# A hybrid decoder layer with experts: a token's expert weights formed in the projection stage, stored beside its row and gathered with it

## The reference

```python
x = _layer_norm(ALPHA * x + (1.0 + g1[:, None]) * mix, ln1_g, ln1_b)
u2 = x * (1.0 + sc2[:, None]) + sh2[:, None]
# _hier_moe, un = u2 as rows
p_group = softmax(g_logits); g_sel = argmax(g_logits)
top_v, top_i = lax.top_k(e_sel, TOP_K)            # e_sel: logits of the chosen group
top_w = softmax(top_v) * take_along_axis(p_group, g_sel[:, None], axis=1)
comb = one_hot(g_sel)[:, :, None] * w_in_group[:, None, :]   # n_tok x 16, two entries not zero
h = jax.nn.silu(hg) * hu * comb[:, :, None]
y = jnp.einsum('nef,efd->nd', h, w_down)
x = _layer_norm(ALPHA * x + (1.0 + g2[:, None]) * y_moe, ln2_g, ln2_b)
```

## Time and profile before

| | us |
|---|---|
| median of 3 runs (lowest, highest) | 1300.3 (1299.82, 1301.27) |
| the profiled execution | 1304.18 |
| its span, first to last instruction | 1302.2 |
| PE busy | 1182.5 (91%) |
| DVE busy | 920.2 (71%) |
| ACT busy | 500.9 (38%) |
| POOL busy | 358.5 (28%) |
| mean granted clock of PE | 0.956 of full speed |

### The profile page before, as it was taken

The page is one execution under the profiler, slowest core; times in us unless marked ns, Lnnn a source line. Parts: engine busy times, 40 slices in busy tenths (PEclk is TensorE's granted clock), DMA queues, the critical chain, the costliest instruction groups (busy, mean ns, idle before and its releaser), DMA issues.

```text
span 1302.2 us, 23073 instructions
## 1 busy us (share of the span) xinstructions
PE 1182.5 (91%) x6683; PEld 963.3 (74%) x6684; DVE 920.2 (71%) x1821; ACT 500.9 (38%) x934; POOL 358.5 (28%) x447
## 2 busy tenths in 40 slices
PE   6889999999999489999997379999999999999495
PEld 2378988988999478888785368888888888888242
DVE  2764988888898689898899875457655745432298
ACT  0525335444533432111111334446544644422175
POOL 1411202212220431211120053344445544332100
PEclk9979999999999699999999589999999999999798
DMA  8814224404413455344333568877998789854673
GB/s 337 293 41 168 66 96 161 141 20 161 161 53 110 150 171 179 130 163 159 130 121 130 182 232 234 236 221 204 302 272 241 211 246 286 250 129 76 211 279 153
DMA packets 112561, 231.44 MB, mean 178 GB/s; under 512 B 11735, under 2 KB 70363, under 8 KB 109419
## 3 DMA queue, kind: packets, MB, share of 16 engines
q1 hardware_dynamic: 98691, 180.50, 39.6%
q0 software_dynamic: 13824, 50.34, 16.5%
HBM read 161.49 MB, written 69.97 MB: 178 GB/s over the span
## 4 chain that ended last, share of the span: by engine, by line
PE 69%; DVE 17%; issue 5%; ACT 4%; DMA 3%; POOL 1%; SPq 1%; DVEq 0%; ACTq 0%; POOLq 0%
PE bank L1599 19%; PE bank L1601 19%; PE bank L1600 19%; PE bank L1552 5%; DMA ada_arena<-in_w_ada 2%; PE bank L1687 2%; DVE ada_arena L1533 2%; PE bank L1573 2%; PE bank L1620 1%; DVE arena L1252 1%; PE bank L1774 1%; DVE ada_arena L1519 1%; DVE st L1255 1%; PE bank L1629 1%; DVE arena L1268 1%
## 5 line engine op out<-in xcount | busy, mean ns | idle before, releaser
L1599 PE MATMUL bank<-parts 128*128 128x256 f32 (+2 forms) x1472 | 513.3, 349 | 38.6 <-ACT arena L775 20.9
L1601 PE MATMUL bank<-parts 128*128 128x256 f32 (+2 forms) x1472 | 496.4, 337 | 0.0
L1600 PE MATMUL bank<-parts 128*128 128x256 f32 (+2 forms) x1472 | 495.9, 337 | 0.0
L1599 PEld LDWEIGHTS bank<-parts 128*128 128x128 f32 x1472 | 283.0, 192 | 82.6 <-ACT arena L775 29.1
L1601 PEld LDWEIGHTS bank<-parts 128*128 128x128 f32 x1472 | 282.7, 192 | 28.6
L1600 PEld LDWEIGHTS bank<-parts 128*128 128x128 f32 x1472 | 283.4, 193 | 25.5
L1552 PE MATMUL bank<-ident,arena 128*128 128x128 f32 (+4 forms) x788 | 116.4, 279 | 14.3 <-DMA arena<-u_d,tok_i 5.8
L1552 PEld LDWEIGHTS bank<-ident,arena 128*128 128x128 f32 (+4 forms) x788 | 94.5, 145 | 39.8 <-issue 9.2
L1442 DVE TENSOR_TENSOR parts<-arena,parts x90 | 105.0, 1221 | 15.9 <-ACT parts L942 14.2
L1454 DVE TENSOR_TENSOR arena<-arena,bank 128x256 f32<-128x256 f32 x48 | 20.1, 419 | 132.3 <-ACT arena L952 131.2
L647 POOL TENSOR_TENSOR arena<-arena 128x256 f32<-128x256 f32 (+1 forms) x36 | 26.1, 728 | 267.9 <-DVE h_last L1181 190.0
(11 more groups left out here) (266 smaller groups left out, 1761.3 us busy)
## 6 DMA issues: line engine op xcount, KB each, us to landing
arena<-in_w_ada SPq DMA_DIRECT2D x16, 1024.0 KB, 8.4
arena<-in_w_gate SPq DMA_DIRECT2D x16, 1024.0 KB, 5.9
arena<-in_w_up SPq DMA_DIRECT2D x16, 1024.0 KB, 12.7
arena<-in_w_down SPq DMA_DIRECT2D x16, 1024.0 KB, 14.5
y_d<-zero SPq DMA_DIRECT2D x17, 512.0 KB, 6.4
ada_arena<-in_w_ada SPq DMA_DIRECT2D x4, 2048.0 KB, 15.4
arena<-in_x_prompt SPq DMA_DIRECT2D x8, 1024.0 KB, 7.8
yT_d<-arena SPq DMA_DIRECT2D x16, 512.0 KB, 4.6
```

Source lines behind the costliest of these rows:

```text
L1599: pe.matmul(out, x_hi, w_hi, start=start, stop=False)
L1600: pe.matmul(out, x_hi, w_lo, start=False, stop=False)
L1601: return pe.matmul(out, x_lo, w_hi, start=False, stop=stop)
```

## The change

A token's 16 expert weights (`comb`, two of them not zero) are formed batch by batch by DVE: `weigh(n)` right after `choose(n)`, the Exp of both softmaxes on ACT in one instruction, and `weights_of(n)` before `rows_of(n)` (for batch 3, which now takes tiles 13 to 16, after it). POOL stores `comb` to DRAM in 16 new columns beside each row of u2, in two DMAs, and waits for both before the first gather. A gathered row has 1040 elements. ACT, in `x_evac`, reads the slot's expert number and copies the one column of `xg` that belongs to it into `wslot` (`w_now`); both `y_evac` wait for that, and so does the gather that overwrites the buffer. `plain_rows`, the three bf16 parts, POOL's three multiplications, PE's 68 matmuls and DVE's sums go. ACT's loop over the tiles of the projection stage is written out. SP stores zeros into the 16 columns of the 128 spare rows. The diff, without plain renaming and address changes:

```diff
+WEIGH = ((0, 4), (4, 5), (9, 4), (13, 4))
...
-        u2_d = nc.dram_tensor("u2_d", [P + NTOK, D], F32).ap()
+        u2_d = nc.dram_tensor("u2_d", [P + NTOK, D + NE], F32).ap()
...
-        prod_w = ada_at(18432, 2, NT, NE)
+        prod_w = ada_at(28300, 2, 5, NE)
...
-        hot_b = at(19072, 2 * NT * SLOTS).bitcast(BF16).rearrange("p (k t v s) -> p k t v s", k=2, t=NT, v=2)
...
+        comb = ada_at(24832, NT, NE)
...
+            sp.dma_start(u2_d[0:P, D:D + NE], zero[:, 0:NE]).then_inc(S["junk_in"], 16)
...
+            pool.wait_ge(S["comb_ok"], len(WEIGH))
+            pool.dma_start(u2_d[P:P + SEQ, D:D + NE].rearrange("(t p) e -> p t e", p=P), comb[:, 0:NT - 1, :]).then_inc(S["comb_st"], 16)
+            pool.dma_start(u2_d[P + SEQ:P + NTOK, D:D + NE], comb[0:NS, NT - 1, :]).then_inc(S["comb_st"], 16)
             pool.wait_ge(S["idx_ready"], 1)
...
-            pool.wait_ge(S["junk_in"], 16)
+            pool.wait_ge(S["junk_in"], 32)
+            pool.wait_ge(S["comb_st"], 32)
             for s in range(2):
                 pool.indirect_dma_start(out=xg[s], out_offset=None, in_=u2_d,
                                         in_offset=bass.IndirectOffsetOnAxis(ap=tok_i[:, s:s + 1], axis=0)).then_inc(S[f"xg{s}"], 16)
-            pool.wait_ge(S["wpart_ready"], 1)
-            by_tok = lambda v: v.unsqueeze(3).to_broadcast([P, 2, NT, SLOTS])
-            for v in range(2):
-                o.did(pool.tensor_tensor(hot_b[:, :, :, v, :], hot_s, by_tok(w_part[v]), ALU.mult))
-            o.wait()
-            pool.tensor_tensor(hot_s, hot_s, by_tok(w_part[2]), ALU.mult).then_inc(S["hotw_ready"], 1)
             for s in (2, 3):
                 pool.wait_ge(S["xgT_mm"], 2 * s - 2)
+                pool.wait_ge(S["w_now"], s - 1)
                 gather(s, s % 2)
...
-            with act.Fori(1, NT // 2 - 1) as j:
-                for b in range(2):
-                    u2T_evac(2 * j + b - 2)
-                    split_y(2 * j + b + 2, b, j + 2)
-                    deviation(2 * j + b, b)
+            def weigh(n):
+                act.wait_ge(S["w_exp"], n + 1)
+                act.activation(exp_in[:, 0:5 * WEIGH[n][1]], exp_in[:, 0:5 * WEIGH[n][1]], ACT.Exp).then_inc(S["w_expd"], 1)
+            for t in range(2, NT - 3):
+                u2T_evac(t - 2)
+                split_y(t + 2, t % 2, t // 2 + 2)
+                deviation(t, t % 2)
+                if t - 1 in CHOOSE_AT:
+                    weigh(CHOOSE_AT.index(t - 1))
             u2T_evac(NT - 5)
             split_y(NT - 1, 0, NT // 2 + 1, NS)
             deviation(NT - 3, 0)
             u2T_evac(NT - 4)
             deviation(NT - 2, 1)
+            weigh(2)
             u2T_evac(NT - 3)
             deviation(NT - 1, 0, NS)
             u2T_evac(NT - 2)
@@ -918,16 +926,12 @@
                 act.activation(u2T[:, 4 * h:4 * h + 4, 0:NS], bank[4 + h][:, :].rearrange("p (k n) -> p k n", n=P)[:, :, 0:NS],
                                ACT.Copy).then_inc(S["u2T_ok"], 1)
+            weigh(3)
...
-            act.wait_ge(S["w_exp"], 1)
-            act.activation(g_dif, g_dif, ACT.Exp).then_inc(S["w_expd"], 1)
-            act.wait_ge(S["w_exp"], 2)
-            act.activation(d_12, d_12, ACT.Exp).then_inc(S["w_expd"], 1)
...
-            def x_evac(s):
+            def x_evac(s, b):
+                e = act.value_load(slot_ei[0:1, 0, ds(s, 1)], min_val=0, max_val=NE - 1)
                 for h in range(2):
                     act.wait_ge(S["xgT_mm"], 2 * s + h + 1)
+                    if h == 0:
+                        act.activation(wslot[:, ds(s, 1)], xg[b][:, ds(e + D, 1)], ACT.Copy).then_inc(S["w_now"], 1)
...
+                act.wait_ge(S["w_now"], s + 1)
...
-            act.wait_ge(S["wslot_ok"], 1)
...
-            def plain_rows(n):
-
-                t0, nt = BATCHES[n]
-                for t in range(t0, t0 + nt):
-                    for k in range(2):
-                        o.did(dve.tensor_scalar(hot_a[:, k, t, :], iota_r[:], pos_f[:, k, t:t + 1], None, ALU.is_equal))
+            def weigh(n):
+                t0, nt = WEIGH[n]
+                tiles = slice(t0, t0 + nt)
+                gl, el = logits[:, tiles, 0:NGR], logits[:, tiles, NGR:NR]
+                g_dif, d_12 = exp_in[:, 0:NGR * nt].rearrange("p (t g) -> p t g", g=NGR), exp_in[:, NGR * nt:5 * nt]
+                o.did(dve.tensor_tensor(prod_w[:, :, 0:nt, :], e_all[:, :, tiles, :], el.unsqueeze(1).to_broadcast([P, 2, nt, NE]), ALU.mult))
+                o.step(dve.tensor_reduce(g_max[:, 0:nt], gl, axis=AX, op=ALU.max))
+                o.did(dve.tensor_tensor(g_dif, gl, bc(g_max[:, 0:nt], NGR), ALU.subtract))
+                o.step(dve.tensor_reduce(m_12[:, :, 0:nt], prod_w[:, :, 0:nt, :], axis=AX, op=ALU.add))
+                dve.tensor_tensor(d_12, m_12[:, 1, 0:nt], m_12[:, 0, 0:nt], ALU.subtract).then_inc(S["w_exp"], 1)
+            def weights_of(n):
+                t0, nt = WEIGH[n]
+                tiles = slice(t0, t0 + nt)
+                g_dif, d_12 = exp_in[:, 0:NGR * nt].rearrange("p (t g) -> p t g", g=NGR), exp_in[:, NGR * nt:5 * nt]
+                dve.wait_ge(S["w_expd"], n + 1)
+                o.step(dve.tensor_reduce(w_sum[:, 0:nt], g_dif, axis=AX, op=ALU.add))
+                o.step(dve.scalar_tensor_tensor(w_sum[:, 0:nt], d_12, 1.0, w_sum[:, 0:nt], ALU.add, ALU.mult))
+                o.step(dve.reciprocal(w_one[:, 0, 0:nt], w_sum[:, 0:nt]))
+                o.step(dve.tensor_tensor(w_one[:, 1, 0:nt], w_one[:, 0, 0:nt], d_12, ALU.mult))
+                o.step(dve.tensor_tensor(prod_w[:, :, 0:nt, :], e_all[:, :, tiles, :], w_one[:, :, 0:nt].unsqueeze(3).to_broadcast([P, 2, nt, NE]), ALU.mult))
+                dve.tensor_tensor(comb[:, tiles, :], prod_w[:, 0, 0:nt, :], prod_w[:, 1, 0:nt, :], ALU.add).then_inc(S["comb_ok"], 1)
...
-                if n < 3:
-                    plain_rows(n)
...
                     choose(CHOOSE_AT.index(t))
+                    weigh(CHOOSE_AT.index(t))
                 if t in rows_at:
+                    weights_of(rows_at.index(t))
                     rows_of(rows_at.index(t))
             router_out(NT - 2)
...
             choose(4)
+            weigh(3)
             rows_of(3)
+            weights_of(3)
             rows_of(4)
...
-            plain_rows(3)
-            plain_rows(4)
-            gl, el = logits[:, :, 0:NGR], logits[:, :, NGR:NR]
-            o.step(dve.tensor_reduce(g_max, gl, axis=AX, op=ALU.max))
-            g_dif3 = g_dif.rearrange("p (t g) -> p t g", g=NGR)
-            dve.tensor_tensor(g_dif3, gl, bc(g_max, NGR), ALU.subtract).then_inc(S["w_exp"], 1)
-            o.step(dve.tensor_tensor(prod_w, e_all, el.unsqueeze(1).to_broadcast([P, 2, NT, NE]), ALU.mult))
-            o.step(dve.tensor_reduce(m_12.rearrange("p (k t) -> p k t", k=2), prod_w, axis=AX, op=ALU.add))
-            dve.tensor_tensor(d_12, m_12[:, NT:2 * NT], m_12[:, 0:NT], ALU.subtract).then_inc(S["w_exp"], 1)
-
...
-            dve.wait_ge(S["w_expd"], 2)
-            o.did(dve.tensor_reduce(w_sum, g_dif3, axis=AX, op=ALU.add))
-            o.step(dve.tensor_scalar(m_12[:, 0:NT], d_12, 1.0, None, ALU.add))
-            o.step(dve.tensor_tensor(w_sum, w_sum, m_12[:, 0:NT], ALU.mult))
-            o.step(dve.reciprocal(wgt[:, 0, :], w_sum))
-            o.step(dve.tensor_tensor(wgt[:, 1, :], wgt[:, 0, :], d_12, ALU.mult))
-            o.step(dve.tensor_copy(w_part[0], wgt[:]))
-            o.step(dve.tensor_tensor(w_rest, wgt[:], w_part[0], ALU.subtract))
-            o.step(dve.tensor_copy(w_part[1], w_rest))
-            o.step(dve.tensor_tensor(w_rest, w_rest, w_part[1], ALU.subtract))
-            dve.tensor_copy(w_part[2], w_rest).then_inc(S["wpart_ready"], 1)
...
+                dve.wait_ge(S["w_now"], s + 1)
...
-            def slot_weights():
-
-                dve.wait_ge(S["wslot_mm"], 1)
-                part_sum = [bank[7][:, n * SLOTS:(n + 1) * SLOTS] for n in range(3)]
-                o.step(dve.tensor_copy(wslot[:], part_sum[2]))
-                o.step(dve.tensor_tensor(wslot[:], wslot[:], part_sum[1], ALU.add))
-                o.step(dve.tensor_tensor(wslot[:], wslot[:], part_sum[0], ALU.add))
-                dve.memset(spare[0:1, 0:1], 0.0).then_inc(S["wslot_ok"], 1)
-
...
-            slot_weights()
...
-            def slot_weights(parts):
-                pe.wait_ge(S["hotw_ready"], 1)
-                for k in range(2):
-                    for t in range(NT):
-                        if parts == 2:
-                            out, w = bank[7][:, 0:2 * SLOTS], hot_b[:, k, t, :, :].rearrange("p v s -> p (v s)")
-                        else:
-                            out, w = bank[7][:, 2 * SLOTS:3 * SLOTS], hot_s[:, k, t, :]
-                        last = pe.matmul(out, hot_a[:, k, t, :], w, start=k == 0 and t == 0, stop=k == 1 and t == NT - 1)
-                return last
-
...
             gate_up(0, 0)
             turn_x(1, 1, 1)
-            slot_weights(2)
```

(7 more changed lines are left out.)

38 lines of the change are left out of this document (19 added, 19 removed).

## The result

The changed kernel takes 1294.38 us (median of 5, 1293.13 to 1294.75); the kernel before, beside it, 1300.56 (1299.82 to 1303.6). The profiled execution took 1293.13 us, its span is 1291.4 us at a mean clock of 0.959.

What follows compares the result with a forecast made beforehand. PE was taken as filled nearly everywhere, with DVE also nearly full in the projection and PE almost empty in the hand-over. First product +0.4 and matmuls -0.6 gave -0.2 us: 1300.1 us, no change, range 1296.0 to 1305.0.

Steps and rivals of the forecast that it cites:

- Step 3: POOL's `comb` store ahead of the first gather: 10.8 us of issue, wait ending at 745.4 us, 3.75 us after `tok_i`.
- Rival B: Store cheap, its wait covered by DVE's placing of tokens: first gate product at 752.45, -3.3 us, 1297.0 us; chance 0.30.
- Step 4: First gate product, where DVE's and ACT's chains meet: starts at 755.6 us instead of 755.17, +0.4 us.
- Step 2: Tail ahead of `tok_i`: `weigh(3)` and `weights_of(3)` on DVE without cover, 0.95 + 1.25 = +2.2 us.
- Step 1: Weights formed by DVE in the projection stage, against `plain_rows` leaving: together +0.4 us at the stage's end.
- Step 5: PE's slot-weight matmuls go between gate products 0 and 1; gate product 1 starts 0.6 us sooner, -0.6 us.
- Step 6: Expert loop: ACT's added register load, `wslot` copy and waits per slot fit in slack and cost nothing.
- Rival D: ACT's table switches between Exp and Sqrt reach the projection's path: +2.6 us on the forecast, 1302.7 us; chance 0.10.

Runs made afterwards that it cites:

- b_loads2: Kernel before, with DVE's three register loads moved between the third and fourth split of expert 0's weights; 1300.67 us, ratio 0.9996.
- a_exposed: Kernel after, with a one-element DVE memset and a wait for its end set between the weight splits and the register loads; ratio 0.9971.
- b_nomm: Kernel before without POOL's three multiplications, PE's 68 slot-weight matmuls and DVE's sums, softmaxes kept, slots weighted with 1; 1300.34 us, ratio 0.9994.
- b_again: Kernel before run once more without an edit, for a second profile; profiled span 1301.2 us.
- b_loads: Kernel before, with DVE's wait for slots_ready and three register loads moved ahead of its four weight splits; 1302.66 us, ratio 1.0009.
- b_none: Kernel before with all forming of slot weights left out, softmaxes included, every slot weighted with 1; 1288.36 us, ratio 0.9891.
- a_noact: Kernel after without ACT's per-slot register load, `wslot` copy and the `w_now` waits, slots weighted with 1; 1293.7 us, ratio 0.994.
- a_late: Kernel after, with the last batch's `weights_of` moved from ahead of `tok_i` to behind it; 1304.25 us, ratio 1.0023.
- a_late2: a_late, with SP's load of expert 1 held back until the first gathered row has landed; ratio 0.9996.

## Why the prediction was wrong

**Step 3, the store and its wait, failed.** I built 10.8 us of issue out of 5.1 ns a piece, from the difference between POOL's scatter and gather. It was 1.41 us. What I took for a price per row there isn't one for a plain store: the queue's packets rose only from 13824 to 13904 between the two profiles, by 80, while the pieces number 2112 and are 64 B each. Landing was 3.9 us after the issue began. My lower bound, 0.96 us, was close. So the wait for the store, which I had ending at 745.4 us and 3.75 us behind `tok_i`, was over 5 us ahead of the gather and cost nothing. The bounds were right; the point between them stood on one difference of two rows, stretched sixteenfold in the number of pieces. Rival B, "the store is cheap", had this part of the mechanism: the gather starts at `tok_i`.

**Step 4, the first product, failed too, and B with it.** B gave 1297.0, since I put gate 0 at 752.45 by DVE's chain and 10.2 us after the gather by ACT's. In the trace gate 0 is 8.7 us after the gather and 6.1 us after `slots_ready` (739.48), where I had 8.25. Both chains were copied from before with an exposed part in them that belonged to their neighbours: DVE's 2.0 us of issue, shown by b_loads2 and a_exposed, and on ACT 1.7 us between the turn and the x copies. The profile puts the second down to PE; in before and b_loads2 it follows the short Exp of L929 (742.37, then the copies at 744.26 in b_loads2) and in the kernels without that Exp it is gone. That it is ACT's three register loads is argued from these rows, not isolated by a run. Together 7.4 us went from `tok_i` to gate 0: 5.3 of DVE's own work that I had listed, and 2.0 of loads. I had listed the 5.3 and then given them away again to the store's wait; the 2.0 I had kept. B, which counted the 5.3 as gone and not the 2.0, was still 2.6 us above the measured time.

**Step 2, the tail, held in its instructions and missed one effect.** Priced +2.2, and `weigh` and `weights_of` took 0.89 and 1.28 us. From L1252 (after: L1259) of tile 16 to `tok_i` it was 27.5 us before and 30.35 after, +2.86; the missing 0.7 is the operation stretched beside the store's issue.

**Step 1, the projection, was about right in its work (+0.4) and wrong in what I allowed for position.** From tile 0 to tile 16 it is -1.8 us, of which tile 5 to tile 8 alone is -2.0, so the work by itself is +0.2; against b_nomm, which has the same stall gone, it is +0.8. One 1.22 us operation of DVE in tile 7 took 3.32 us before, because POOL had started its subtraction 0.2 us earlier. DVE and POOL before:

```profile
578.12 3.32 DVE L1252 SCALAR_TENSOR_TENSOR arena<-arena 128x1024 f32<-128x1024 f32 x1
```
```profile
577.93 2.42 POOL L670 TENSOR_TENSOR parts<-arena,parts 128x1024 fp32r<-128x1024 f32 x1 [12.85 <-ACT parts L815]
```

and after:

```profile
574.90 1.22 DVE L1259 SCALAR_TENSOR_TENSOR arena<-arena 128x1024 f32<-128x1024 f32 x1
```
```profile
575.38 3.04 POOL L670 TENSOR_TENSOR parts<-arena,parts 128x1024 fp32r<-128x1024 f32 x1 [13.50 <-ACT parts L816]
```

Here DVE started first, and POOL's operation took the longer time. b_nomm dodges the same stall (DVE 1.22 us, started 0.03 us ahead of POOL, whose operation then took 3.49) without any of the change's work in this stage, so the 2 us are luck of position and no merit of the change. I had named the mechanism and its 2 us, but widened the range by 1 us. b_again, b_loads and b_loads2 have the stall like the kernel before, and b_none and all eight traces of the later code dodge it: both kernels that were profiled twice repeat it.

**Step 5, the slot-weight matmuls, held.** From the start of x(1)'s turn to gate 1 it is 3.2 us and was 3.76: -0.55, forecast -0.6. In b_nomm, without ACT's new copy, it is 2.9. What that gives is below what the clock between gate 0 and gate 1 varies by, so it shows in no time.

**Step 6, the expert loop, held as to cost** (a_noact; PE's idle time in the loop is 0.2 us and was 1.3), while the loop is 2 us shorter in the traces for a reason that stays open. **Rival D** fell: ACT loads the tables ahead of its waits, and DVE's longest wait for the root stayed at 0.3 us.

```profile
575.32 1.28 ACT L896 ACT_TABLE_LOAD   x1
577.92 0.20 ACT L896 ACTIVATE sd<-mv 128x1 f32<-128x1 f32 x1 [1.32 <-DVE mv L1267]
```
```profile
DVE rs L1269 <- ACT sd L896: 4.3, 16, 0.3
```

The Trainium skill's 2.66 us a switch ("ScalarE: Activation LUTs", What ACT_TABLE_LOAD costs) had no place to show here: ACT was waiting anyway.

Summed by steps, in the traces: store and first product -7.4 where I had -2.2 (gate 0 +0.4 in all, with `tok_i` +2.6), tail +2.9 for +2.2, projection -1.8 for +0.4, loop -2.6 for 0 (-2.0 by the means of the two families). Of the gain, the 7.4 us have a cause that the runs show; the 2 us of the projection are luck, and the 2 of the loop have no known cause.

## What to carry to other kernels

When work leaves a chain, price what is left by its own instructions, and ask of each idle time in it which neighbour exposes it: an idle time with "issue" behind short instructions can vanish together with them. An unknown cost whose bounds are sixteenfold apart is two forecasts, not one in the middle. And a small transfer on the critical path should be issued ahead of the bulk load that it would run beside, also where that load is on another queue: what delays it by some microseconds can put it behind megabytes (a_late against a_late2).
